# One change to a two-block transformer kernel in float32 on one core: attention scores on all 128 rows, the first feed-forward block in seven products

## What is computed

```python
def swiglu_ffn(x, norm, w_gate, w_up, w_down):      # 1024 -> 2816 -> 1024
    h = rms_norm(x, norm)
    return (silu(h @ w_gate) * (h @ w_up)) @ w_down

# mixer, branch A (4 heads, two parts c each, keys up to the query's chunk)
s = einsum('bqhcd,bkhcd->bhcqk', q, k) * 64 ** -0.5
w = p[:, :, 0] - lam * p[:, :, 1]                    # p = softmax(s)
# mixer, branch B (8 heads of 64, relative bias), branch C (retention)
s = einsum('bnqhd,bnkhd->bnhqk', q, k) * scale + bias
# second part: 8 heads of 64, local windows and dilations as one bias table
```

## Time and profile before

| what | value |
|---|---|
| runs, median of three | 3177.75 us |
| the profiled execution's own time | 3178.9 us |
| its span, first to last instruction | 3177.1 us |
| TensorE, matmuls | 3142.0 us busy (99%), 15170 matmuls |
| VectorE | 1921.4 us (60%) |
| ScalarE | 1539.5 us (48%) |
| GpSimd | 374.1 us (12%) |
| mean granted TensorE clock | 0.997 of full speed |
| transfers | 469.19 MB, mean 148 GB/s |

### The profile page before, as it was taken

The page is one execution under the profiler, slowest core; times in us unless marked ns, Lnnn a source line. Parts: engine busy times, 40 slices in busy tenths (PEclk is TensorE's granted clock), DMA queues, the critical chain, the costliest instruction groups (busy, mean ns, idle before and its releaser), DMA issues.

```text
span 3177.1 us, 37772 instructions
## 1 busy us (share of the span) xinstructions
PE 3142.0 (99%) x15170; PEld 2586.5 (81%) x15170; DVE 1921.4 (60%) x3038; ACT 1539.5 (48%) x2388; POOL 374.1 (12%) x403
## 2 busy tenths in 40 slices
PE   9999999999999999999999999999999999999998
PEld 7889877778888888888977777888889877788887
DVE  6564777644455556645687755455465767766545
ACT  5453547643344435534456754345353455454434
POOL 2111010000012111112020100001120100012210
PEclk9999999999999999999999999999999999999999
DMA  9985332323289878878342322368894654179872
GB/s 289 241 207 133 99 102 67 100 80 93 93 216 251 200 161 206 208 179 210 98 116 73 93 87 79 94 189 198 205 217 102 110 91 70 61 207 243 197 172 69
DMA packets 329537, 469.19 MB, mean 148 GB/s; under 512 B 17297, under 2 KB 221457, under 8 KB 329361
## 3 DMA queue, kind: packets, MB, share of 16 engines
q1 hardware_dynamic: 254608, 331.92, 34.7%
q0 software_dynamic: 74608, 134.77, 23.8%
q10 hardware_dynamic: 144, 0.10, 0.0%
HBM read 458.32 MB, written 2.10 MB: 145 GB/s over the span
## 4 chain that ended last, share of the span: by engine, by line
PE 93%; DVE 5%; ACT 1%; DMA 0%; issue 0%; SPq 0%; DVEq 0%; ACTq 0%
PE bank L596 28%; PE bank L608 15%; PE bank L601 15%; PE bank L610 13%; PE bank L603 13%; PE bank L1428 2%; PE bank L1076 2%; PE bank L1477 1%; PE bank L1461 1%; DVE k_wl L818 1%; PE bank L1271 1%; PE bank L1720 1%; PE bank L1611 0%; PE bank L2217 0%; DVE k_qkva L1312 0%; DMA k_xraw<-in_ffn_w_gate 0%
## 5 line engine op out<-in xcount | busy, mean ns | idle before, releaser
L818 DVE TENSOR_TENSOR k_wl<-k_raw,k_wh 128x1024 fp32r<-128x1024 f32 (+1 forms) x315 | 369.9, 1175 | 420.5 <-ACT k_wh L810 419.3
L810 ACT ACTIVATE k_wh<-k_raw 128x1024 fp32r<-128x1024 f32 (+1 forms) x315 | 320.5, 1018 | 436.2 <-PE bank L608 286.4
L818 DVE TENSOR_TENSOR k_wl<-k_xraw,k_wh 128x1024 fp32r<-128x1024 f32 (+1 forms) x278 | 317.9, 1143 | 268.7 <-ACT k_wh L810 267.3
L810 ACT ACTIVATE k_wh<-k_xraw 128x1024 fp32r<-128x1024 f32 (+1 forms) x278 | 276.2, 994 | 388.4 <-PE bank L608 221.0
L596 PE MATMUL bank<-k_xh,k_wh 128*128 128x512 f32 x840 | 356.3, 424 | 0.0
L608 PE MATMUL bank<-k_xh,k_wl 128*128 128x512 f32 x840 | 328.9, 392 | 1.1 <-DVE k_wl L818 1.1
L601 PE MATMUL bank<-k_xl,k_wh 128*128 128x512 f32 x840 | 328.1, 391 | 0.0
L596 PE MATMUL bank<-k_h,k_wh 128*128 128x512 f32 x696 | 271.8, 391 | 0.0
L608 PE MATMUL bank<-k_h,k_wl 128*128 128x512 f32 x696 | 271.1, 390 | 0.0
L601 PE MATMUL bank<-k_h,k_wh 128*128 128x512 f32 x696 | 271.0, 389 | 0.0
L596 PE MATMUL bank<-k_wh,k_S 128*128 128x512 f32 (+1 forms) x656 | 246.4, 376 | 0.0
(11 more groups left out here) (381 smaller groups left out, 6678.5 us busy)
## 6 DMA issues: line engine op xcount, KB each, us to landing
k_raw<-in_w_in SPq DMA_DIRECT2D x153, 512.0 KB, 3.6
k_xraw<-in_ffn_w_up SPq DMA_DIRECT2D x88, 512.0 KB, 7.4
k_xraw<-in_ffn_w_gate POOLq DMA_DIRECT2D x56, 512.0 KB, 8.0
k_xraw<-in_ffn_w_down SPq DMA_DIRECT2D x53, 512.0 KB, 6.2
k_xraw<-in_ffn_w_gate SPq DMA_DIRECT2D x48, 512.0 KB, 5.9
k_xraw<-in_ffn_w_up POOLq DMA_DIRECT2D x36, 512.0 KB, 10.3
k_xraw<-in_ffn_w_up SPq DMA_DIRECT2D x46, 384.0 KB, 4.3
k_raw<-in_w_out SPq DMA_DIRECT2D x28, 512.0 KB, 3.4
```

Source lines behind the costliest of these rows:

```text
L810: e.activation(self.pair[c.pair][0][:, 0:n], self.unit[c.src][:, 0:n], ACT.Copy).then_inc(*self.act.up(("wh", c.i)))
L818: e.tensor_tensor(lo[:, 0:n], self.unit[c.src][:, 0:n], hi[:, 0:n].bitcast(F32), ALU.subtract).then_inc(*self.dve.up(("wl", c.i), ("split" ...
```

## The change

It does five things.

1. Block 0 of each feed-forward stage is made by the seven products too. `ORDER` is the new order of the products. Block 0's share two more banks with block 1's. `pe_plain`, `act_plain` and `dve_plain` go. The sums of the input, and the norm, have earlier due times.
2. T3, and in blocks 2 to 5 also T1, are no longer made by transfers: VectorE subtracts B11 and B22 from T2 (`mix`, `dve_mixes`), behind the split of T2 for P6. In stage 0 block 0's T1 and T2 are also added on VectorE.
3. Scores: q's high and low half stand one over the other in 128 rows (`q0`, `q1` for the two heads), k's high half and k's low half are each laid out twice, over both row halves. A burst is four matmuls with 128 rows (`stacked`), (high + low of q) x high of k, then x low of k, for each head.
4. `pool_stack`: eight transfers from SBUF to SBUF for each tile, on GpSimd's queue, bring the halves there. `act_halves` waits for the stack of the tile before, since the halves are made in one staging buffer. The splits are due 6, 9, 7.5 and 7.5 steps before their scores in "a" and "b", 3.5 steps before the first in "m2".
5. Due times of some other steps are moved, among them the rotation of branch C, head norms, gates, the bias signs and the state-space heads; the load of the constants waits until tick 40; loads of the input are taken one weight piece later.

The core of the diff:

```diff
+def product_order():
+    out = [(0, "P1"), (1, "P1"), (0, "P2"), (0, "P6"), (1, "P2"), (0, "P7"), (0, "P5"), (0, "P4"), (0, "P3"), (1, "P6"), (2, "P1"),
+           (1, "P7"), (1, "P5"), (1, "P4"), (1, "P3")]
...
+        if b == 1:
+            out[begin3]["loads"].append((b, "T3", "B12"))
+            out[begin3]["adds"].append((b, "T3", "B22"))
+            at("P1")["gone"].append((b, "B11"))
+        else:
+            at("P6")["post"].append((b, "T3", "T2", "B11", ALU.subtract, "B11"))
+        if b > 1:
+            out[begin1]["loads"].append((b, "B22", "B22"))
+            at("P6")["loads"].append((b, "T1", None))
+            at("P6")["post"].append((b, "T1", "T2", "B22", ALU.subtract, None))
...
+    def mix(self, e, x, n):
+        out, a, b, op, waits, key = x
+        for ref in waits:
+            e.wait_ge(*self.sig(ref))
+        e.tensor_tensor(self.unit[out][:, 0:n], self.unit[a][:, 0:n], self.unit[b][:, 0:n], op).then_inc(*self.dve.up(key))
...
-        yield self.at[st]["start"] + (12.5 if st else 26.6)
+        yield self.at[st]["start"] + 12.5
...
-        t = self.at[st][0, "B12"] + 6.4 + 9.8 * q
+        t = self.at[st]["start"] + (0.5 if st else 0.0)
+        return {"d": t + 5.0 + 6.5 * q, "s": t + 6.8 + 6.5 * q, "S3": t + 6.8 + 6.5 * q, "s2": t + 2.5 + 6.5 * q, "S2": t + 9.5 + 6.5 * q,
...
     def act_halves(self, e, st, kind):
...
+            if t:
+                e.wait_ge(*self.steps[f"stack{(t - 1) % 2}"].sig((st, kind, t - 1, 7)))
+            elif kind == "b":
+                e.wait_ge(*self.steps["stack1"].sig((st, "a", 3, 7)))
+            e.activation(qq[:, 0:T], q, ACT.Copy).then_inc(*self.act.up(("qh", st, kind, t)))
+            e.activation(kk[:, 0:T], k, ACT.Copy).then_inc(*self.act.up(("kh", st, kind, t)))
...
+    def pool_stack(self, e, st, kind):
...
+            yield self.half_tick(a, t) + 3.0
+            e.wait_ge(*self.dve.sig(("kl", st, kind, t)))
...
+            landed, n = self.steps[f"stack{t % 2}"], 0
+            for s, (dst, rows) in enumerate(((q0, low), (q1, high))):
+                for to, part in ((low, qq[:, 0:T]), (high, qq[:, T:2 * T])):
+                    e.dma_start(dst[to, :], part[rows, :]).then_inc(*landed.up((st, kind, t, n)))
+                    n += 1
+                for to in (low, high):
+                    e.dma_start(self.KK[kind][t][s][to, :], kk[rows, :]).then_inc(*landed.up((st, kind, t, n)))
+                    n += 1
+
+    def stacked(self, e, outs, q, k, qcols, n, marks):
+
+        for s in range(2):
+            for i in range(2):
+                x = e.matmul(outs[s], q[s][:, qcols], k[s][:, i * T:i * T + n], start=i == 0, stop=i == 1, skip_group_check=True)
+        x.then_inc(*self.pe.up(*marks))
...
-                e.wait_ge(*self.dve.sig(("kl", st, kind, t)))
+                e.wait_ge(*self.steps[f"stack{t % 2}"].sig((st, kind, t, 7)))
...
-        start, end = at["start"] + 58.6, at["xbc"][1].at + 8.0
+        start, end = at["start"] + 60.5, at["xbc"][1].at + 7.6
```

511 lines of the change are left out of this document (257 added, 254 removed), and 3 rows, old and new, of the table at.

## The result

The changed kernel takes **3172.66 us** (median of 20 runs, 3169.63 to 3175.22), the kernel before 3178.8 (median of 20, 3175.31 to 3180.66). The ratio is 0.9981, 95% interval 0.9975 to 0.9988: 6 us faster. The forecast was 3135, its range 3120 to 3157: the measured time is 37.7 us above the forecast and outside the range.

What follows compares the result with a forecast made beforehand. TensorE's row of matmul starts was taken as the bound. From 3178.9 us: 27.2 less for products, 18.4 less for scores, 1 more for heads, 2 more for stacks gave 3136.3, or 3135 against the median; range 3120 to 3157.

Steps and rivals of the forecast that it cites:

- Part 1: First feed-forward block in seven products instead of four plain pieces: 120 matmuls fewer over five stages, 27.2 us less.
- the 343 that the prediction set as its test: Feed-forward stages, 347 us before: the forecast is wrong if they last more than 343 us.
- The cost of nothing for VectorE's work in the blocks: Feed-forward blocks: added subtractions and splits hide behind the ring of four operand pairs, costing nothing; 84 us without that cover.
- The heads at 1 us more in all: Feed-forward stage heads, where input sums are needed sooner: 1 us more together, between 3 less and 12 more.
- Part 2: Attention scores: bursts of four full-row matmuls cost 50.4 us instead of 68.8, 18.4 less; bounds 22.8 less to 14.6 more.
- The rival of the gaps: Score bursts keep their 0.41 us gaps, making scores 14.6 us slower: 3168 us, or 3151 with half; chance 0.08.
- the rule of packing taken alone: Scores: packed bursts count three steps against four, so the change would lose 12.6 us there, 3166 in all.
- Part 3: Mixers' stacking transfers: landing 3.0 us, 7 us from split to score; fits in stages 1 and 4, 2 us more overall.
- The prediction's own sign, each mixer shorter by about 7 us: Mixers: the forecast is wrong if a mixer isn't shorter by about 7 us.
- Stage 6, 2 us more: First score of stage 6: due at 2527.5, its stack lands at 2529.8; 2 us more, between 0 and 6.
- Late operands: Stacks 2 to 3 us late in several tiles, input sums late in stage heads: 20 us more, 3155; chance 0.10.
- the sum as it stood: Whole kernel: all terms added, 3135 us against the median, own range 3120 to 3146; chance 0.72.

Runs made afterwards that it cites:

- Four homes: Changed kernel with, in stage 6 alone, splits written in place, half the stacks' bytes and space for two more alibi tables, loaded one pair ahead: 3165.59 us.
- first pairs in place: Changed kernel with each attention's first pair of heads writing row-keeping halves directly, only row-changing copies transferred (0.79 MB, not 1.57): 3164.67 us.

## Why the prediction was wrong, by its steps

- **Part 1, 120 matmuls of 0.227 us: right.** The four feed-forward stages behind the first are 342.8, 342.7, 343.3 and 342.2 us, against the 343 that the prediction set as its test (one of them misses it by 0.3). Taking the products back costs these stages 17 us. Of the 5.45 us per stage 4.3 arrive; 0.7 of the rest is the wait for ScalarE's drain (L1127) in each head. The cost of nothing for VectorE's work in the blocks held: no wait for a split (L870) over 1 us in a feed-forward stage but the first.
- **The heads at 1 us more in all, at most 12: the step that failed first.** The opening and stage 0 alone missed by 14.2 us. I took the bound from the free time between due times and didn't look at VectorE's queue from 20 to 60 us, where the rows of before show how full it was: 13.8 and 16.4 of 20 us. I called 13.2 the fullest stretch I had looked at. The six sums (L851) of 1.22 us were added there. What the runs showed in its place: in this stretch TensorE waits 9.3 us more, and its clock is at half for 13.7 us in place of 3.4, some 5.1 us more. That is the miss, 14.4 us. The prediction had no term for the clock. By cause, the runs give 4 us to the parameters' chain in its old place and 3 to 4.5 to four of the sums, each with its share of the clock. Which of VectorE's or ScalarE's work makes the other 6 or 7 us was not taken apart.
- **Part 2, 18.4 us less for the scores: right in mechanism, 16.8 in size.** The 256-key burst costs 0.49 and the 384-key one 0.72, within 0.04 of the forecast. The new bursts never change shape and no gap is left in them, which agrees with the reason the prediction gave; that the old gap came from the change of shape and not from the pairs that run together was not tried apart. The rival of the gaps falls. So does the rule of packing taken alone, by which the prediction had the change lose 12.6 us: the Trainium skill, TensorEngine Tiling (Array Packing), "Theoretical Speedup", gives up to 2x for a dimension of 64 or less, and here the packed bursts cost 68.8 us against 52.0.
- **Part 3, stacks landing in 3.0 us: the step that failed second.** I took the landing time of a 256 KB table, loaded where the DMA share was 0.39 to 0.93, for the last of eight transfers in a row beside weights, where it was 1.24. It measured 7.1 us. "Split 3 us and transfers 7 us just fit" became 11.7 from split to score, plus VectorE making the split 4.4 us after ScalarE, behind the rotations. With the first stacks cut to half, stages 1 and 4 give back 6.3 us and stage 6 some 3. The prediction's own sign, each mixer shorter by about 7 us, did not come: stages 1 and 4 are shorter by 0.9 and 1.7. Whether it is the loads of weights beside them or the row of eight that makes the stacks slow was not tried apart. The upper bound should have been a transfer's time in a stretch where the DMA engines are full.
- **Stage 6, 2 us more:** the wait was 4.24, and a second one (3.77) came from a load that I had called early enough: the tables' transfers start when the maxima allow it, and there is no slack to be had by due times. Four homes took it away. The half clock, 10.2 us where it was 3.4, costs 3.4 us more.
- **Late operands**, the rival with 0.10, was the right one in kind. Of the two places it named, the stacks were late, though only the first of stages 1, 4 and 6. The sums of the input in the stage heads were not what TensorE waited for: its waits there are for splits of weights in stage 0, and of 0.7 us for a drain in the others. It priced the whole at 20 us and gave 3155, with one late pair of 2.4 us in the opening, where 14 us were lost. The chance of 0.72 for the sum as it stood was too high for a change that adds waits in three stages on in-order queues.
- **Not settled:** of the 12.1 us in stages 1 and 4, 8.1 are TensorE's added waits (7.1 of them for the first stacks) and 1.3 the size of the bursts. Some 2.7 us stay unexplained, less than kernels with the same code differ by in these stages. Nor was it tried what the opening takes with all of VectorE's additions away.

## What to carry to other kernels

Cost a new transfer by its place: what else is under way there, how many are issued in a row, and what waits for the last of them. A transfer's median in a less full stretch is its lower bound. Before adding work to an in-order engine, read how full it is in the tightest stretch it is added to, above all the opening, and move what nobody waits for (a chain of tiny operations, a norm's parameters) into the middle of a stage with room, since at the next stage's head it costs as much again. When a wait names a releaser, look at what that engine had waited for itself. Where a new wait can halve TensorE's clock, count that too: here it was 8.5 us of a miss of 37.

## What the runs showed of the hardware

- An elementwise operation of VectorE on 64 rows takes as long as on 128: 687 and 688 ns for 512 columns. So two operations that are split by rows into four take twice as long.
- Two 64-row matmuls issued together, six in a burst, cost more than four on all rows, one after the other (68.8 against 52.0 us for 80 bursts), though the six are only three steps of time.
- TensorE's granted clock can fall to half (1.2 of 2.4 GHz, starts 0.43 apart for 512 columns) at a wait. In the changed kernel it was so for 3.4 us from 12.2, 6.8 us from 39.5, 3.4 us from 53.1, 3.4 from 452.5 and 1677.9, 6.8 from 2524.4 and 3.4 from 2589.2, each time with a wait of 2.8 to 4.3 us at that point (the first time 2.3 us earlier). A stretch of 3.4 us costs some 1.7 us. How long it lasts, and with waits of 2.2 us whether it comes at all, differs between kernels: at the wait of 2.2 us in the head of stage 1 the clock was halved for 3.4 us in the kernel before, for 6.8 us in the one with first pairs in place, and not in the changed kernel. From 40 to 60 us the changed kernel's mean is 0.76, and 0.92 in the kernel with the parameters' chain moved; from 20 to 40 us it is the other way round, 0.99 and 0.91.
- Transfers within SBUF of 256 KB took 5.8 us to land (median of the first group; 4.7 to 7.5 in the others) when eight (1.57 MB) were issued in a row beside the loads of weights. The Trainium skill, DMA: Bandwidth & Descriptors, "Anatomy of one DMA — SWDGE (gpsimd) path", has about 2.0 us plus the bytes at 436 GB/s, by which I estimate 2.6 us for 256 KB and 5.6 for the whole stack in one. The table's 3.0 us is near the first; the stack's 10.7 us from first issue to last landing is twice the second, so here the measurement decides.
